# Borders around the latent-attention projections: later store waits, query latents prepared earlier, fewer sum products

## The reference, cut to what matters

```python
hn = rmsnorm(h, norm1_g) * (1 + sc1) + sh1          # latent and context tokens
p = split(hn @ w_in)                                 # query latents 512, key/value latents 256, rotary key 64, and others
q = rmsnorm(q_lat, q_norm) @ w_uq                    # 6 heads of 128 + 64
c_kv = rmsnorm(kv_lat, kv_norm); k = c_kv @ w_uk; v = c_kv @ w_uv
mla = softmax(q k^T / sqrt(192)) v                   # 512 queries, 768 keys
# the mLSTM has per-head gates i, f; exp(-m_t) is the floor of its denominator
```

## Time and profile before

| | us |
|---|---|
| median of 3 runs | 2828.61 |
| lowest, highest | 2825.7, 2834.22 |
| profiled execution, device time | 2836.02 |
| its span | 2834.4 |
| its mean granted TensorE clock | 0.977 |

### The profile page before, as it was taken

The page is one execution under the profiler, slowest core; times in us unless marked ns, Lnnn a source line. Parts: engine busy times, 40 slices in busy tenths (PEclk is TensorE's granted clock), DMA queues, the critical chain, the costliest instruction groups (busy, mean ns, idle before and its releaser), DMA issues.

```text
span 2834.4 us, 31067 instructions
## 1 busy us (share of the span) xinstructions
PE 2717.9 (96%) x12122; PEld 2088.3 (74%) x12122; DVE 1201.2 (42%) x1220; ACT 741.5 (26%) x818; POOL 193.4 (7%) x197
## 2 busy tenths in 40 slices
PE   5999999999999997998999999999999999999996
PEld 3788888887544444786788888888888888888785
DVE  5535533661623367334444333344334433334334
ACT  3222111222223224122323212223122322222221
POOL 1000000100024245000000000000000000000000
PEclk9999999999979999999999999999999999999998
DMA  9765555873160432422222232222232222322222
GB/s 358 283 245 200 200 202 206 317 279 134 37 144 15 131 89 68 166 89 89 74 90 103 81 101 100 104 89 77 100 105 95 97 90 92 104 100 89 84 83 100
DMA packets 97692, 369.04 MB, mean 130 GB/s; under 512 B 21712, under 2 KB 35072, under 8 KB 67128
## 3 DMA queue, kind: packets, MB, share of 16 engines
q1 hardware_dynamic: 72752, 278.26, 29.0%
q0 software_dynamic: 10880, 72.55, 6.8%
q10 hardware_dynamic: 14000, 17.44, 1.7%
HBM read 346.48 MB, written 21.74 MB: 130 GB/s over the span
## 4 chain that ended last, share of the span: by engine, by line
PE 58%; DVE 1%; DMA 0%; issue 0%; ACT 0%; DVEq 0%; ACTq 0%
PE f_ps L2020 57%; PE f_ps L2033 1%; DVE h L2009 0%; DMA f_raw<-in_w_out 0%; DMA h<-in_xT 0%; DVE f_lo L1891 0%; DVE f_square_sum L2006 0%; ACT f_hi L1793 0%; DVE h L1908 0%; DVE f_square_sum L1915 0%; ACT f_val L1799 0%; PE f_pn L2066 0%; PE f_pn L2047 0%; ACT f_val L1812 0%; DVE f_val L1899 0%
## 5 line engine op out<-in xcount | busy, mean ns | idle before, releaser
L2020 PE MATMUL f_ps<-x_hi,f_hi 128*128 128x512 f32 x1632 | 641.5, 393 | 9.3 <-DVE f_lo L1891 7.4
L2020 PE MATMUL f_ps<-x_hi,f_lo 128*128 128x512 f32 x1632 | 643.5, 394 | 0.0
L2020 PE MATMUL f_ps<-x_lo,f_hi 128*128 128x512 f32 x1632 | 642.2, 394 | 0.0
L1891 DVE TENSOR_TENSOR f_lo<-f_raw,f_hi 128x2048 fp32r<-128x2048 f32 (+1 forms) x166 | 337.8, 2035 | 110.9 <-ACT f_hi L1793 98.2
L2020 PEld LDWEIGHTS f_ps<-x_hi,f_hi 128*128 128x128 f32 x1632 | 307.9, 189 | 80.0 <-issue 7.5
L1793 ACT ACTIVATE f_hi<-f_raw 128x2048 fp32r<-128x2048 f32 (+1 forms) x167 | 284.2, 1702 | 292.9 <-PE f_ps L2020 285.6
L2020 PEld LDWEIGHTS f_ps<-x_lo,f_hi 128*128 128x128 f32 x1632 | 307.9, 189 | 71.0
L2020 PEld LDWEIGHTS f_ps<-x_hi,f_lo 128*128 128x128 f32 x1632 | 307.7, 189 | 68.6
L2020 PE MATMUL f_ps<-f_u_hi,f_hi 128*128 128x512 f32 x704 | 277.5, 394 | 4.9 <-DVE f_u_lo L1971 4.9
L2020 PE MATMUL f_ps<-f_u_lo,f_hi 128*128 128x512 f32 x704 | 276.7, 393 | 0.0
L2020 PE MATMUL f_ps<-f_u_hi,f_lo 128*128 128x512 f32 x704 | 276.4, 393 | 0.0
(11 more groups left out here) (270 smaller groups left out, 2917.3 us busy)
## 6 DMA issues: line engine op xcount, KB each, us to landing
f_raw<-in_w_up SPq DMA_DIRECT2D x88, 1024.0 KB, 4.7
i_ring<-in_ada_rest POOLq DMA_DIRECT2D x64, 1024.0 KB, 5.2
f_raw<-in_w_down SPq DMA_DIRECT2D x64, 704.0 KB, 4.1
i_raw<-in_w_in SPq DMA_DIRECT2D x38, 1024.0 KB, 4.8
i_ring<-in_ada_first SPq DMA_DIRECT2D x32, 1024.0 KB, 7.4
f_raw<-in_w_out SPq DMA_DIRECT2D x16, 1024.0 KB, 4.8
g_ring<-rrow SPq DMA_DIRECT2D x24, 256.0 KB, 4.0
i_raw<-in_w_first POOLq DMA_DIRECT2D x16, 320.0 KB, 5.2
```

The costliest lines, as they stand in the source:

```text
L1891: nc.vector.tensor_tensor(w_lo[s][:, 0:kt, :], raw[s][:, 0:kt, :], w_hi[s][:, 0:kt, :].bitcast(F32), ALU.subtract).then_inc(lo_ok, 1)
L2020: mm = nc.tensor.matmul(pt[s][:, :], w[s][:, k, :], v[:, c, :], start=(k == 0 and n == 0), stop=(k == len(slots) - 1 and n == 2))
```

## The change

The waits for the stores leave the end of ACT's list in `stage_front`; their list `ends` goes to SP in `stage_mla`, between the loads of `kr` and of `rope`. The clearing of the spent semaphores moves to the same place, ahead of `rope` and `ident`. The scaling and squaring of the query latents moves from ACT's list in `stage_mla` to that of `stage_front`, ahead of the last tile's evacuation (`take(act, 37)`), into buffers of their own. DVE adds the four squared slices there (three additions), and adds the two slices of the keys in `stage_mla`; PE then sums 4 + 2 matmuls instead of 16 + 4. ACT computes the two floors behind the reading of jobs "v" 0 and "v" 1, and PE transposes the gate columns behind job "v" 3. SP stores the rows ahead of the floors. Buffers move in the arena: the second `wr` tile now lies where the front stage's store buffers were, so POOL's copies into it wait for `r_ld` at 160, that is for all loads of SP up to `ident`.

```diff
 build_program
+        qg=ground.at("a_q_g_times", [P, 4, SEQ], QG_AT), sums=ground.at("a_square_sums", [P, SEQ], SUMS_AT)
 stage_front
+    ends += [(v_st, 16 * len(VU))] + [(stored[s], 16 * done[s]) for s in range(2)]
 stage_front, scalar
                 for u in range(REST):
+                    if u == REST - 1:
+                        act.wait_ge(mod_ok, 2)
+                        act.wait_ge(lat["q_ld"], 16)
+                        for k in range(Q_LORA // P):
+                            nc.scalar.activation(lat["qg"][:, k, :], lat["ql"][:, k, :], ACT.Copy, scale=lat["gq"][:, k:k + 1]
+                                                 ).then_inc(lat["qg_ok"], 1)
+                        act.wait_ge(lat["qg_ok"], Q_LORA // P)
+                        nc.scalar.activation(lat["ql"][:, :, :], lat["ql"][:, :, :], ACT.Square).then_inc(lat["sq_ok"], 1)
                     take(act, u)
...
-                act.wait_ge(v_st, 16 * len(VU))
-                for s in range(2):
-                    act.wait_ge(stored[s], 16 * done[s])
 stage_front, vector (behind sc_ffn)
+                dve.wait_ge(lat["sq_ok"], 1)
+                for k in range(1, Q_LORA // P):
+                    if k >= 2:
+                        dve.wait_ge(lat["qs_ok"], k - 1)
+                    nc.vector.tensor_tensor(lat["sums"][:, 0:SEQ], lat["ql"][:, 0, :] if k == 1 else lat["sums"][:, 0:SEQ],
+                                            lat["ql"][:, k, :], ALU.add).then_inc(lat["qs_ok"], 1)
 stage_mla, sync
                         sp.dma_start(kr[n][32 * m:32 * m + 32, :], pairs[(n + m) % 2]).then_inc(r_ld, 16)
+                for e in ends:
+                    sp.wait_ge(*e)
+                for s in spent:
+                    sp.sem_clear(s)
                 sp.dma_start(rope[:, :, :], A["rope"]).then_inc(r_ld, 16)
                 sp.dma_start(ident[:, :], A["ident"]).then_inc(r_ld, 16)
-                for s in spent:
-                    sp.sem_clear(s)
-                (em stores first, then rrow stores)
+                (rrow stores first, then em stores)
 stage_mla, gpsimd
                 for n in range(2):
+                    if n == 1:
+                        pool.wait_ge(r_ld, 160)
 stage_mla, scalar
-                act.wait_ge(q_ld, 16)
-                for k in range(QK):
-                    nc.scalar.activation(qg[:, k, :], ql[:, k, :], ACT.Copy, scale=gq[:, k:k + 1]).then_inc(qg_ok, 1)
-                act.wait_ge(qg_ok, QK)
-                nc.scalar.activation(ql[:, :, :], ql[:, :, :], ACT.Square).then_inc(sq_ok, 1)
...
-                act.wait_ge(m_ok, 1)
-                nc.scalar.activation(emr[0:4, :], M[0:4, CTX:TOK], ACT.Exp, scale=-1.0).then_inc(em_ok, 1)
-                nc.scalar.activation(emr[32:36, :], M[32:36, CTX:TOK][:, ::-1], ACT.Exp, scale=-1.0).then_inc(em_ok, 1)
+                    if (kind, n) == ("v", 0):
+                        act.wait_ge(r_ld, 160)
+                        act.wait_ge(m_ok, 1)
+                        nc.scalar.activation(emr[0:4, :], M[0:4, CTX:TOK], ACT.Exp, scale=-1.0).then_inc(em_ok, 1)
+                    if (kind, n) == ("v", 1):
+                        nc.scalar.activation(emr[32:36, :], M[32:36, CTX:TOK][:, ::-1], ACT.Exp, scale=-1.0).then_inc(em_ok, 1)
 stage_mla, vector (behind the memset of gb)
+                dve.wait_ge(sq_ok, 2)
+                nc.vector.tensor_tensor(sqk[:, 0, :], sqk[:, 0, :], sqk[:, 1, :], ALU.add).then_inc(kv_ok, 1)
 stage_mla, tensor
-                        pe.wait_ge(sq_ok, 1)
+                        pe.wait_ge(qs_ok, QK - 1)
                         for t in range(QT):
-                            for k in range(QK):
-                                mm = nc.tensor.matmul(sum_ps[0][:, t:t + 1], ql[:, k, t * P:(t + 1) * P], ones[:, 0:1],
-                                                      start=(k == 0), stop=(k == QK - 1), skip_group_check=True)
+                            mm = nc.tensor.matmul(sum_ps[0][:, t:t + 1], sums[:, t * P:(t + 1) * P], ones[:, 0:1],
+                                                  start=True, stop=True, skip_group_check=True)
                         mm.then_inc(ss_ok, 1)
-                        (pe.wait_ge(sq_ok, 2), then two matmuls for each of sqk[:, 0] and sqk[:, 1])
+                        pe.wait_ge(kv_ok, 1)
+                        (two matmuls, on sqk[:, 0] alone)
...
-                pe.wait_ge(c_ok, 4)
-                (six transposes of cnat behind the last job)
+                    if (kind, n) == ("v", KEYT - 3):
+                        pe.wait_ge(c_ok, 4)
+                        (the six transposes of cnat)
```

More of the change, by code:

```diff
@@ L114 @@
 T_X = 142976
+QG_AT = 139264
+SUMS_AT = 137216
 def build_program(nc, A, out):
@@ L161, in front_sem @@
             return spent[-1]
-        stage_front(nc, A, sb, ps, front_sem, sem, proj, vtok, ones, eps, mod, bias_ada, g1col, g2col, gfcol, sc_ffn, lat)
-        stage_mix(nc, A, sb, ps, sem, proj, vtok, mix, ones, eps, front, spent, lat, early)
+        ends = stage_front(nc, A, sb, ps, front_sem, sem, proj, vtok, ones, eps, mod, bias_ada, g1col, g2col, gfcol, sc_ffn, lat)
+        stage_mix(nc, A, sb, ps, sem, proj, vtok, mix, ones, eps, front, spent, ends, lat, early)
         stage_tail(nc, A, out, ground, ps, sem, ones, eps, mod, sc_ffn, gfcol, early)
@@ L173, in stage_front @@
     ORDER = (0, 2, 1, 3, 4)
+    ends = []
     with ExitStack() as ctx:
@@ L719, in _ @@
                 product(pe, KT + 2, 1, False)
+    return ends
 SM_AT = 58368
@@ L731, with stage_mix @@
 ORDER_R = (4, 5, 0, 1, 2, 3)
-def stage_mix(nc, A, sb, ps, sem, proj, vtok, mix, ones, eps, front, spent, lat, early):
+def stage_mix(nc, A, sb, ps, sem, proj, vtok, mix, ones, eps, front, spent, ends, lat, early):
     rrow = nc.dram_tensor("rrow", [2 * ML_H, KEYT, SEQ], F32, kind="Internal").ap()
@@ L755, in stage_mix, with stage_mla @@
         rows_st = sem("l_rows_stored")
-        mla = stage_mla(nc, A, arena, ps, sem, proj, ones, eps, ident, rqs, rows_st, front, spent, ml, lat)
+        mla = stage_mla(nc, A, arena, ps, sem, proj, ones, eps, ident, rqs, rows_st, front, spent, ends, ml, lat)
         stage_heads(nc, A, arena, ps, sem, proj, vtok, mix, ident, rqs, rows_st, mla, ml, na, early)
-def stage_mla(nc, A, arena, ps, sem, proj, ones, eps, ident, rqs, rows_st, front, spent, ml, lat):
+def stage_mla(nc, A, arena, ps, sem, proj, ones, eps, ident, rqs, rows_st, front, spent, ends, ml, lat):
     ccol, rrow, em = ml["ccol"], ml["rrow"], ml["em"]
@@ L773, in stage_mla @@
     v = arena.at("a_v", [P, KEYT, MLA_H * MLA_V], 39936)
-    qg = arena.at("a_q_g_times", [P, QK, SEQ], 58368)
-    sqk = arena.at("a_kv_sq", [P, KK, TOK], 66560)
-    rk = arena.at("a_kv_rstd", [P, TOK], 72704)
+    qg, sums, qg_ok, sq_ok, qs_ok = (lat[n] for n in ("qg", "sums", "qg_ok", "sq_ok", "qs_ok"))
+    sqk = arena.at("a_kv_sq", [P, KK, TOK], 64512)
+    rk = arena.at("a_kv_rstd", [P, TOK], 70656)
     wk = arena.at("a_w_uk", [P, KK, MLA_H * NOPE], 75776)
@@ L780, in stage_mla @@
     rope = arena.at("a_rope", [P, 2, TOK], 88064)
-    wr = [arena.at(f"a_w_rope{n}", [P, QK, MLA_H, ROPE], 129664 + 6144 * n) for n in range(2)]
-    kr = [arena.at(f"a_kr_in{n}", [P, TOK], 141952 + 3072 * n) for n in range(2)]
+    wr = [arena.at(f"a_w_rope{n}", [P, QK, MLA_H, ROPE], (58368, 196416)[n]) for n in range(2)]
+    kr = [arena.at(f"a_kr_in{n}", [P, TOK], 129664 + 3072 * n) for n in range(2)]
     t1 = arena.at("a_t1", [P, TOK], 148096)
@@ L847, in _ @@
                     sp.dma_start(em[4 * d:4 * d + 4, :], emr[32 * d:32 * d + 4, :]).then_inc(rows_st, 16)
-                sp.wait_ge(r_ok, 2 * KEYT)
-                for d in range(2):
-                    sp.dma_start(rrow[4 * d:4 * d + 4, :, :], R[32 * d:32 * d + 4, :, :]).then_inc(rows_st, 16)
             @block.gpsimd
@@ L1048, in _ @@
                     mm.then_inc(up, 1)
-                pe.wait_ge(c_ok, 4)
-                for st in range(KEYT):
-                    mm = nc.tensor.transpose(c_ps[:, st * 36:(st + 1) * 36], cnat[:, st * P:(st + 1) * P], ident[0:36, 0:36])
-                mm.then_inc(ct, 1)
+                    if (kind, n) == ("v", KEYT - 3):
+                        pe.wait_ge(c_ok, 4)
+                        for st in range(KEYT):
+                            mm = nc.tensor.transpose(c_ps[:, st * 36:(st + 1) * 36], cnat[:, st * P:(st + 1) * P],
+                                                     ident[0:36, 0:36])
+                        mm.then_inc(ct, 1)
         front.close()
```

23 lines of the change are left out of this document (12 added, 11 removed).

## The result

The changed kernel takes 2811.22 us (median of 5 runs, 2808.07 to 2815.02) where the kernel before took 2828.61 (5 runs by now, 2824.73 to 2834.22); the ratio is 0.9935, with a 95% interval of 0.9919 to 0.9952. The profiled execution took 2808.07 us, against 2836.02: 28 us apart, where the medians are 17.4 apart.

A forecast was written before the change was run, and what follows sets the result against it. PE, busy 96% of the span, was taken to bound the kernel. From the profiled 2836.0 us, 8.0 for both borders and 17.9 for the attention's clock were subtracted: 2810.1, forecast 2810 us, own range 2804 to 2816, with rivals 2802 to 2819.

The forecast's parts named there:

- Step 1: Front stage to projections: without the store wait the block opens 1.9 us earlier; PE's gap is 1.5 us, not 5.04.
- Step 2: Projections' first two jobs and square sums: jobs take 6.9 us, sums shrink, PE done near 713.0 instead of 725.85.
- Step 3: Projections' job 2: PE idles from 713.0 to 718.8 for ACT's reading, then 2.4 us clock loss; 4.6 us saved.
- Step 4: Work moved inside the projections: floors cost nothing; 52 clears ahead of the rotary loads fit 14.8 us of slack.
- Rival (d): Projections: clears hold up the rotary loads, PE stalls 8 us before the "qr" jobs, about 2820 us; chance 0.04.
- Step 5: Projections to attention: floors and stores gone from the end, PE's gap 1.4 us; 8.0 us saved up to here.
- Step 6: Start of the attention: after only 1.4 us of PE rest the clock holds in most executions; 17.9 us saved.
- Rival (a): Start of the attention: the clock falls all the same, 2828 us, or 2820.6 against the median; chance 0.09.
- (b): Start of the attention: the long half-clock stay is particular to the profiled execution, timed ones lose 2.4 us; 2818.2; chance 0.06.
- (c): Whole kernel: the profiled execution is 7.4 us longer for other reasons, timed ones lose the full 17.9; 2802.7; chance 0.05.

The follow-up runs named there:

- the kernel with reads ahead: Changed kernel with ACT reading jobs 0 and 1 ahead of the gate functions and job 2 ahead of the two roots: 2800.72 us, ratio 0.9883.
- The rest filled: Four unread PE products ahead of the attention: in the kernel before, 2818.42 us; in the changed kernel with four idle ACT copies, 2812.44 us (2823.55 without the products).
- the two borders alone: Kernel before with only the edits between projections and attention: 2813.86 us; changed kernel with those edits undone, leaving the edits between front stage and projections: 2822.77 us.
- the kernel with all rows used: Kernel before with the first attention's rotary score products contracting over all 128 rows instead of 64, which changes its values: 2800.36 us.

## Why the prediction was right

The time of 2810 stands beside 2811.2, and the steps beside these:

- **Step 1.** PE's rest at the first border: 1.5 predicted, 1.60 measured. ACT's early work was hidden in its wait for the last tile.
- **Step 2.** Two jobs in 709.28 - 702.34 = 6.94 us, as predicted (6.9). The sums took 2.3 us where 2.4 were counted. (The working divides 5.31 by 12 and writes 0.43; it is 0.44. It also calls PE busy throughout the half clock from 705.0 to 711.8, where its row has 4.75 of 6.80 us. Nothing hangs on either.)
- **Step 3.** The new wait: 5.8 predicted, 6.12 measured, with ACT's reading as its end. The half clock behind it lasted 3.6 us of work, not 4.8, so it cost 1.8 us and not 2.4. The two errors partly cancel, and a stay behind such a rest, 2.9 to 6.2 us over the profiles, could as well have cost 3. The lower bound of the sum, gate rows that land earlier without `rope` in their company, did not occur (10.43 us against 10.40). But the kernel with reads ahead shows that this step could have been a choice: 7.9 us lay in an order on ACT's list that the change left alone.
- **Step 4.** About 52 clears, and the waits for the stores ahead of them, took 711.19 - 707.48 = 3.7 us, at most 0.07 each, against the 0.28 from which they would have cost. POOL's second eight copies, released by `ident`, were done at 718.8; the rotary jobs started at 733.35. Rival (d) had 14.5 us of slack left. By the price that the Trainium skill ("Advanced Engine Details and Errata", section "Network/Comms") gives for reading a semaphore, taken for a clear, the estimate was 2.6 to 5.2 us; the trace agrees with 3.7.
- **Step 5.** From the last front product to the attention: 94.58 - 86.18 = 8.4 us saved, 8.0 predicted. Its last piece was over-priced, a rest of 1.4 us against 1.16: the barrier took 0.31 us here (786.61 to 786.92), not 0.54.
- **Step 6.** The attention's length: 139.70 - 121.82 = 17.9 us, as predicted from the pace at either clock. Rival (a), a fall of the clock all the same, did not occur in any of 9 profiles with 1.14 or 1.16 us of rest, but did with 2.04 us. The reason given was weaker than it looks. The two nearest rests, 1.8 us that kept the clock and 1.7 us that lost it, were told apart by the products around them; over all profiles the first lost it in 4 of 14 and the second in 6 of 13, so each was one throw. The products behind the 1.7 us have 96 rows, not 64, and the clock came back after 3.4 us there. What carried the step is that the rest became 1.16 us, shorter than either; a rest of the predicted 1.4 us ahead of the attention was not measured.
- **Against which time.** The forecast rested on the claim that the profiled execution lost 17.9 us and the timed ones about 11. The rest filled gains 12.5 us in the kernel before and 11.1 in the changed one, and other profiles show stays of 20 to 23 us. With its interval (8 to 16 us) the first of these gains puts (b), hardly any loss in the timed runs, and (c), the full 17.9, both out. The working held against (b) that the spread of 8.5 us has no other place as large. That was no evidence: with the loss gone the changed kernel still spreads over 7.0 us, and the front stage alone varied by 3.9. What does bear it out is the granted clock: beside the experiments the kernel before took 2836.7 us at a mean clock of 0.977 and 2824.7 at 0.981, and 0.004 of 2834 us is 11 us. The spread is one of half clock, though not of this stage alone.

What the steps account for in the profiled executions is 8.4 + 17.9 of the 28 us. Another 1.3 us is a front stage that ended that much earlier, its half clock near 40 us having lasted 6.8 us and not 10.2, and 0.4 lie behind the attention. Neither comes from the change.

The medians of the two borders alone don't add up exactly: 17 and 8 us under their own before, 25 together, against 18.4 by the changed kernel's ratio. The intervals are 8, 5 and 9 us wide, and the second stay at half clock, beside the one-column sums at 718.6, is missing in some profiles of kernels that kept those sums. How much of the two gains is that, stays open.

The Trainium skill, in "TensorE: Matmul & The Clock Gate", Part 1, has sustained activity release the throttle soon. For products over 128 rows the profiles agree (2.9 to 6.2 us after PE resumed). For the attention's mix with 64-row products none does: 20 to 38 us. The measurement decides, and the kernel with all rows used shows that it is the 64-row products among them that matter, by their rows or by the changes of height that they bring.

## What to carry to other kernels

Price a rest of PE by the clock behind it, and look at which products come next: ahead of products of 128 and 64 rows in turn a rest of 2 to 5 us cost 10 to 18 us more than itself, ahead of dense work 1.5 to 3. Put products of one height side by side. Where the rest can't be removed, a few products that nobody reads bridge it. And when a border is shortened, ask at once what is late next; here an evacuation queued behind an unrelated chain on ACT took over, and reordering that list was worth half as much as the whole change.

## What the runs showed of the hardware

- Half clock was kept for 20, 23 and 38 us of continuously busy PE where half of the products had 64 contraction rows, and ended after 3.7 us where all had 128. Whether it is the rows or the changes of height stays open.
- Products of 128 and of 64 rows in turn cost 0.17 to 0.20 us for each change of height: 3.97 us a unit with four changes, 3.58 with two, 3.24 with none.
- Rests of 1.16 us ahead of the attention and of 1.60 us at the first border left the clock at 1.00 in every profile that has them (9 each); 2.04 us ahead of the attention and 3.36 at the first border did not. In between it depended on the execution: half clock followed 1.70 us in 6 of 13 profiles and 1.83 us in 4 of 14.
- The clock fell without a rest of PE amid 32 records of one moving column, at 714.4 in the kernel with the sums on PE; other kernels with the same records kept it.
- About 52 semaphore clears took SP at most 3.7 us.
